# Filler products on the tensor engine while it waits in the routing and between the layers

## The reference, cut to what matters

```python
g_logits = einsum('bld,dg->blg', h, wg) + bg            # 4 groups
g_idx = argmax(g_logits)                                 # one group per token
e_sel = e_logits of that group                           # 4 experts in it
top_v, top_i = top_k(e_sel, 2)                           # two experts per token
w_k = softmax(top_v) * g_w
hid = silu(h @ w1[e]) * (h @ w3[e])                      # 1024 -> 256
out = (hid * gate) @ w2[e]                               # 256 -> 1024
x = x + ga2 * out
```

## Time and profile before

| | us |
|---|---|
| median of three runs | 814.08 |
| lowest and highest | 810.16, 819.76 |
| the profiled execution, its own time | 812.59 |
| its span in the trace | 810.7 |
| PE busy | 682.2 |
| mean granted clock of PE, share of full | 0.927 |

### The profile page before, as it was taken

How to read it: one execution, slowest core, us unless ns; L and a number is a source line. 1 busy time by engine, 2 the same in 40 slices (tenths; PEclk the granted TensorE clock), 3 DMA queues, 4 the chain that set the end, 5 groups by cost and what they waited for, 6 DMA issues and landing times.

```text
span 810.7 us, 9627 instructions
## 1 busy us (share of the span) xinstructions
PE 682.2 (84%) x3623; PEld 390.0 (48%) x3624; DVE 233.9 (29%) x485; ACT 140.8 (17%) x288; POOL 176.2 (22%) x232
## 2 busy tenths in 40 slices
PE   2788999999957998799679898788899489999940
PEld 0334444554545663466244553345445456666620
DVE  1200312222171322122350323355312712322315
ACT  2201000001111221121030211245112021221201
POOL 4000011110421222112130100456423112222212
PEclk9899999999966999999979999999999579999985
DMA  9999797593082999998684502914201749979934
GB/s 342 391 343 359 303 367 311 201 405 122 26 308 71 417 423 420 421 391 338 243 346 188 214 19 85 397 72 154 121 12 61 277 184 412 364 272 422 421 149 183
DMA packets 52618, 213.95 MB, mean 264 GB/s; under 512 B 13984, under 2 KB 21152, under 8 KB 33392
## 3 DMA queue, kind: packets, MB, share of 16 engines
q1 hardware_dynamic: 31520, 178.59, 55.2%
q0 software_dynamic: 10240, 24.38, 8.4%
q10 hardware_dynamic: 10832, 10.63, 4.0%
HBM read 207.57 MB, written 15.43 MB: 275 GB/s over the span
## 4 chain that ended last, share of the span: by engine, by line
PE 68%; DMA 20%; DVE 5%; issue 3%; ACT 1%; SPq 1%; ACTq 1%; POOL 0%; POOLq 0%; DVEq 0%
PE ps L1298 13%; PE ps L1235 10%; DMA pool<-in_mod_w 7%; PE ps L1323 7%; PE ps L1371 7%; DMA pool<-in_moe_w 6%; PE ps L1414 5%; PE ps L1172 4%; PE ps L1388 3%; PE ps L1531 3%; DMA pool<-h_rows,of_now 2%; PE ps L1282 2%; PE ps L1459 2%; DMA pool<-y_rows 2%; PE ps L1225 1%
## 5 line engine op out<-in xcount | busy, mean ns | idle before, releaser
L1298 PE MATMUL ps<-pool 128*64 128x256 f32 x1280 | 149.0, 391 | 7.1 <-issue 4.6
L1298 PEld LDWEIGHTS ps<-pool 128*64 128x64 f32 x1280 | 107.7, 142 | 53.2 <-issue 22.0
L1235 PE MATMUL ps<-pool,yT 128*128 128x512 f32 x192 | 84.6, 595 | 0.0
L1323 PE MATMUL ps<-pool 128*64 128x512 f32 x320 | 74.7, 608 | 5.3 <-DMA pool<-in_moe_w 2.8
L1172 PE MATMUL ps<-pool,cs 128*32 128x512 f32 x384 | 49.7, 651 | 23.6 <-DMA pool<-in_mod_w 13.4
L1371 PE MATMUL ps<-hT,pool 128*128 128x384 f32 x192 | 66.0, 498 | 0.0
L1235 PEld LDWEIGHTS ps<-pool,yT 128*128 128x128 f32 x192 | 35.7, 190 | 41.3 <-issue 41.1
L534 POOL TENSOR_SCALAR pool<-pool 128x384 f32<-128x384 f32 (+1 forms) x36 | 36.6, 1032 | 76.6 <-DVE pool L1102 76.5
L1371 PEld LDWEIGHTS ps<-hT,pool 128*128 128x128 f32 x192 | 37.4, 199 | 31.4 <-issue 10.3
L932 DVE SCALAR_TENSOR_TENSOR pool<-ps,pool 128x256 f32<-128x256 f32 x20 | 9.7, 484 | 129.3 <-PE ps L1298 129.3
L1323 PEld LDWEIGHTS ps<-pool 128*64 128x64 f32 x320 | 25.4, 139 | 40.7 <-issue 38.9
(11 more groups left out here) (218 smaller groups left out, 792.8 us busy)
## 6 DMA issues: line engine op xcount, KB each, us to landing
pool<-in_moe_w SPq DMA_DIRECT2D x96, 1024.0 KB, 13.6
pool<-in_mod_w SPq DMA_DIRECT2D x24, 2048.0 KB, 10.3
pool<-in_ev_w_in SPq DMA_DIRECT2D x6, 1024.0 KB, 20.0
pool<-in_ev_w_in SPq DMA_DIRECT2D x2, 2048.0 KB, 24.0
ga<-mods POOLq DMA_DIRECT2D x8, 512.0 KB, 7.5
pool<-in_ev_w_out SPq DMA_DIRECT2D x2, 2048.0 KB, 10.5
pool<-mods POOLq DMA_DIRECT2D x8, 512.0 KB, 8.5
pool<-in_od_w_out SPq DMA_DIRECT2D x2, 2048.0 KB, 9.6
```

Of the source, the lines that this page charges most:

```text
L1235: ins = mm(ps[:, 2 * t + n, :], yT[:, k, t * P:(t + 1) * P], weight(parts[k // 4], 4, D)[:, k % 4, n * 512:n * 512 + 512], start=k == 0, s ...
L1298: ins = mm(ps[m, k, 0:DE], hTe.rearrange("p (c n) -> p c n", c=DC)[:, cc, m], w[e][:, cc, :], start=cc == 0, stop=cc == DC - 1)
L1323: ins = mm(ps[m, 4 + n, :], hidT[:, cc, m], w2[e][:, cc, n * 512:n * 512 + 512], start=cc == 0, stop=cc == 1)
```

## The change

A helper `keep_clock(n, bank)` multiplies the identity with 512 columns of the constant table into a bank that nobody reads, n times. It is called at four places on PE's stream: three times over before the wait for the mask, four before the wait for the first one-hot table (none before the second), two before the wait for the gathered rows (these three in both layers), and nine before the norm's transposes at the transition. Nothing else is changed.

```diff
+            def keep_clock(n, bank):
+                for _ in range(n):
+                    mm(ps[:, bank, :], ident, cst[:, C_CS2:C_CS2 + 512], start=True, stop=True)
+
             def rank_tokens(l):
+                keep_clock(3, 1)
                 pe.wait_ge(*L(l, "mask", 1))
...
                 for v in range(2):
+                    keep_clock((4, 0)[v], 1)
                     pe.wait_ge(*L(l, "onehot", v + 1))
...
                 step_contents(l)
+                keep_clock(2, 1)
                 pe.wait_ge(S(f"L{l}_gathered"), 16)
                 turn_rows(range(DC))
...
             for part in range(4):
                 mod_part(1, 1, part)
+            keep_clock(9, 6)
             norm_transposes(1)
```

## The result

The changed kernel took 809.0 us (median of 17 runs, 800.7 to 812.2) against 811.4 for the kernel before, run beside it as often (806.4 to 819.8). The ratio is 0.9928, interval 0.990 to 0.9956: 5.8 us less, 3.6 to 8.1. The ratio is not taken from the two medians, which lie only 2.4 us apart (the means 5.1). Four executions among those of the experiments, of 1229 to 2338 us, count in none of them.

A forecast was written before the change was run, and what follows sets the result against it. PE was taken as the bound, slowed where its clock falls to 1.2 GHz in both routings and the transition. Terms summed to -2.7 - 2.5 - 0.5 = -5.7 us, giving 806.9 or 808.4; forecast 808, range 802 to 815.

The forecast's parts named there:

- (a): Three fillers before the mask: start at 1.2 GHz, overrun the 4.04 us wait, on the path; +1.0 us (+0.3 to +1.2).
- (b): Twelve ranking records after the mask: 1.4 us instead of 2.75 if the clock is up; -1.1 us (0 to -1.35).
- (c): Four fillers before the first one-hot table: 3.5 us at full clock, hidden in the 4.88 us wait; mostly free, +0.2 us.
- (d): Twelve 20-column products after the first one-hot table, on the path: faster if the clock lasts; -0.9 us (0 or -1.35).
- (e): Two fillers before the gathered rows: free at full clock, 3.5 us at half against a 2.49 us wait; +0.5 us.
- (f): Eight transposes of the gathered rows: 1.97 us at half clock, 1.1 at full; -0.2 us (0 to -0.9).
- (g): First expert step: clock back before it, 7.11 us instead of 9.65 in layer 0; -2.2 us (0 to -2.54).
- (h): Expert loop of layer 0: loads set the pace but start when the first step frees slots, so the gain passes through.
- (i): Nine fillers in the transition: no delay, faster transposes, projection then held by first tile's columns and weight landing; gain 0.5 us.
- strong rival: Everything at full clock: first batch wakes it and it never falls again in the routing; about -12 us, 802; chance 0.14.
- even case: Fillers pay for themselves and no more, starting at half clock and ending late; -2 to +2 us, 812 to 816; chance 0.21.
- slower one: Fillers never wake the clock, each batch served at 1.2 GHz; +4.4 us a layer, +9.4 in all, 823; chance 0.05.

The follow-up runs named there:

- again: The changed kernel itself, unaltered, timed and profiled once more: ratio 0.9887 to the kernel before, 9.2 us below.
- routing only: The changed kernel without the nine fillers in the transition, those of the routing kept: ratio 0.9909 to the kernel before, 7.4 us less.
- router one: The changed kernel with one filler more, ahead of the router's last batch: ratio 0.9908 to the kernel before.
- full: The changed kernel with one filler before the router's last batch, four before mask, six and one before one-hot tables, four before rows, twelve in transition: 0.9862 to before.
- thin: The changed kernel with each 512-column filler replaced by four of 16 columns: ratio 1.0087 to the kernel before, 7.1 us slower.
- last four: The changed kernel with four fillers in place of two ahead of the gathered rows: ratio 0.9901 to the kernel before, 8.0 us below.
- no first: The changed kernel without the three fillers ahead of the mask: ratio 0.9968 to the kernel before, 2.6 us below.
- no last: The changed kernel without the two fillers ahead of the gathered rows: ratio 0.9971 to the kernel before, 2.4 us below.
- transition only: The kernel before with only the nine fillers in the transition added: ratio 0.9998 to the kernel before.

## Why the prediction came out

The time, 809.0 against 808, and the change, -5.8 us against -5.7, agree. The first agreement is in part luck: 808 was reckoned from a median of 814.1 for the kernel before, which in the timed set was 811.4, and the set's own medians differ by only 2.4 us. Term by term, by the profile of layer 0, it is less close:

- (a) First batch. Predicted +1.0; the ranking started 4.50 us after the router's end in place of 4.04, +0.5, and between +0.1 and +0.7 in the five other stretches of the same code (change, again, routing only). The clock came back inside it, as said. The batch is worth far more than (a) and (b) say, since without it the later ones meet their waits at the wrong clock.
- (b) Ranking 1.4 us for 2.75: -1.3 against -1.1.
- (c) Four fillers hidden, 1.52 us of the wait left: within 0.2, as said.
- (d) The first table's products 1.51 us: -1.2 against -0.9.
- (e) The last two ran at 1.2 GHz, 3.76 us: rows' transposes 0.7 us late in layer 0, 0.0 in layer 1, against +0.5.
- (f) -0.2, as said.
- (g) First step 7.13 in all six stretches of the change and routing only: -2.5 against -2.2. This is the term on which I had hedged, for runs where the clock comes too late; none did.
- The sum is -3.9 us in layer 0 and -4.2 in layer 1 where -2.7 and -2.5 stood. The mechanism was right and (a), (d) and (g) were sized too cautiously, each by 0.3 to 0.5 us in layer 0; in layer 1 it was (a), (b), (c), (d) and (e), of which (c) and (e) cost nothing there. The working has two slips that did not decide anything: by its own terms layer 1's sum is -2.4, and the -12 that sets the low end of the range is the strong case, not the half-strong one (-9).
- (h) The gain passes through layer 0's loads: yes on average, though not in full in this profile. Layer 0's expert loop took 128.9 us before and 130.5 after, so it ended 1.2 us earlier where its first step ended 2.8 earlier. From the end of the first step's up-projections to the end of the modulation products it was 137.4 and 137.3 us in the two profiles without fillers in the routing, and 136.4 to 139.1, 137.3 on average, in the twelve with them. The two longest, this one (139.1) and router one (138.9), had 11 us at 1.2 GHz in it, all others 0 or 5.5. The stretch behind the gain did not grow by it.
- (i) Transition -0.5: right, 14.81 for 15.32 us, and for the reason given: the projection waited 0.77 us for its weights, issued at 407.23, 7.2 us before it began.

The stages thus say -8.7 us. The timed sets say -5.8 (3.6 to 8.1) and -9.2 (6.1 to 12.3). The agreement of the first with -5.7 is in part luck too: a stage gain larger by 3 us, and a set that showed less of it. In the profiled execution the missing part is in the attention, as shown above. That falls of the clock elsewhere differ from one execution to the next, in kernels whose code there is the same, is shown (in the ten profiles without the extra filler of router one that stretch took 211.2 to 217.8 us). For the difference between the two sets the granted clock of each execution speaks: the changed kernel spent 85.6 us at 1.2 GHz on average in the first set (mean time 807.5 us) and 78.6 in the second (805.1), and within each set a further microsecond at 1.2 GHz goes with 0.3 us of time, which makes 2.1 of the 2.4 us. Why the clock fell more often in one set stays open, and the rest of the difference is the kernel before, whose mean was 812.6 and 814.7.

The strong rival (all at full clock, -12) did not come with this change: the clock fell again before the last batch in all six stretches. The version full got -11.2, with the clock up all through one of its two routings. The even case and the slower one did not come; thin is what the slower one looks like.

The statement of the Trainium skill that full clock does not engage for transposes ("TensorE: Matmul & The Clock Gate", Part 4) is contradicted a second time. In last four the clock fell at 406.0 and was back at 409.4 (0.64 in 408:410), with only transposes on PE from 405.35 on and the projection at 410.15:

```profile
405.35 4.57 PE L1190 MATMUL ps<-cst,xn 128*128 128x128 f32 x24 [2.34 <-DVE xn L758]
410.15 2.41 PE L1422 MATMUL ps<-pool,hT 128*128 128x512 f32 x5 [0.23 <-DMA pool<-in_od_w_in]
```

```profile
408.00:410.00 2.00, 1.91 (x11) 1.72 (x9) 2.00 (x7) 1.86 (x7) 1.70 (x4) 0.64 0.93 394
```

## What to carry to other kernels

Filler products in a wait pay where slow work follows on the path: here a first expert step 2.3 to 2.5 us shorter and two sets of thin products 2.6 us shorter together, for 0.6 to 1.3 us of delay. They paid next to nothing where a load and other engines were next: in the transition about 0.6 us of the stage, and nothing that the timed runs could tell. Length matters at both clocks: two fillers that left 1.7 us of their wait empty at full clock did not keep it up, and four that overran the wait by 3 us, mostly at half clock, cost 1.8 us a layer. Taking one batch away can leave the work behind a later one slower than with none (10.05 us for 9.65).

## What the runs showed of the hardware

- Products of 16 columns kept PE and its weight loads busy without a gap for 7 us and left the clock at 1.2 GHz; for 34 us of such work and waits it did not return (thin, 226.6 to 260.7). With products of 512 columns in the same places it was back 4.1 and 4.4 us after the first batch began (the change, 231.27 to 235.3 and 633.67 to 638.1).
- Two fillers at full clock with a pause of 1.7 us and eight transposes behind them did not hold it (no first, fall at 250.2 us), and the first step, begun 0.85 us after the fall, took 10.05 us, 0.4 more than with no fillers.
- The same code in the attention took 211 to 218 us from profile to profile, with the clock at 1.2 GHz for 4 us of it in the shortest (again) and 22 us in the longest (no first, no last, transition only).
- Between the fillers and the transposes of the transition the clock stayed up in both profiles of the change (pauses of 2.3 and 1.9 us; 1.00 in 400:412 and 395:409), and in last four it fell at 406.0, 0.7 us after a pause of 2.3 us.
